# LayerNorm statistics in a one-core streaming encoder step: the variance by a product of ones, rstd from exp(-ln/2) and a Newton step

## What is computed

```
proj   = rms_norm(x) @ W_in                       # 1024 -> 3584, split into h,b,c,z (a) and a,g,z (b)
out_a  = b_a * conv3(c_a * h_a) * silu(z_a)       # 512 channels
conv_b = conv31(a_b * sigmoid(g_b)) + bias        # 512 channels
s_b    = silu(layer_norm(conv_b) * g + b)         # over the 512 channels
y      = x + concat(out_a, s_b * silu(z_b)) @ W_out
return rms_norm(y), and the last rows of both convolutions' inputs
```

## Time and profile before

| what | value |
|---|---|
| median of 3 runs | 1513.71 us (1513.64 to 1514.19) |
| the profiled execution | 1513.34 us |
| its span, first to last instruction | 1511.5 us |
| mean granted TensorE clock | 0.999 of full speed |
| busy: PE, DVE, ACT, POOL | 1500.0, 1306.0, 593.5, 652.7 us |

### The profile page before, as it was taken

The page is one execution under the profiler, slowest core; times in us unless marked ns, Lnnn a source line. Parts: engine busy times, 40 slices in busy tenths (PEclk is TensorE's granted clock), DMA queues, the critical chain, the costliest instruction groups (busy, mean ns, idle before and its releaser), DMA issues.

```text
span 1511.5 us, 19728 instructions
## 1 busy us (share of the span) xinstructions
PE 1500.0 (99%) x7114; PEld 1323.5 (88%) x7114; DVE 1306.0 (86%) x1333; ACT 593.5 (39%) x986; POOL 652.7 (43%) x569
## 2 busy tenths in 40 slices
PE   9999999999999999999999999999999999999998
PEld 8999999988888888888888888889898778888885
DVE  7899999999998898899899895798898788888875
ACT  7553432433342343333253322124444344444433
POOL 4887778311424232342432351116654544444441
PEclk9999999999999999999999999999999999999999
DMA  6897968688988889998789888767867755455541
GB/s 250 308 356 286 366 248 323 213 305 302 319 292 292 278 283 334 306 343 283 257 276 320 299 269 261 247 209 209 247 217 230 257 189 177 169 184 193 171 152 70
DMA packets 119512, 388.97 MB, mean 257 GB/s; under 512 B 17848, under 2 KB 23096, under 8 KB 115832
## 3 DMA queue, kind: packets, MB, share of 16 engines
q1 hardware_dynamic: 116872, 387.57, 74.9%
q10 hardware_dynamic: 2544, 0.14, 0.1%
HBM read 279.19 MB, written 108.47 MB: 256 GB/s over the span
## 4 chain that ended last, share of the span: by engine, by line
PE 97%; DVE 1%; DMA 1%; POOL 0%; issue 0%; ACT 0%; SPq 0%; POOLq 0%; DVEq 0%; ACTq 0%
PE ps L2399 32%; PE ps L2401 32%; PE ps L2400 32%; PE ps L2521 0%; PE ps L2514 0%; DMA conv_b<-conv_spill 0%; DMA x_raw<-in_xT 0%; PE ps L2605 0%; PE ps L2609 0%; DVE conv_b L2177 0%; DVE h_rows_odd L2332 0%; POOL w_ring_f L1302 0%; PE ps L2507 0%; DVE h_rows_even L2325 0%; PE ps L2508 0%
## 5 line engine op out<-in xcount | busy, mean ns | idle before, releaser
L2137 DVE SCALAR_TENSOR_TENSOR ps<-v,conv_b_taps,ps 128x920 f32<-128x920 f32 (+2 forms) x580 | 630.7, 1087 | 17.3
L2399 PE MATMUL ps<-xf,w_ring 128*128 128x460 f32 (+1 forms) x1624 | 603.4, 372 | 0.3 <-issue 0.3
L2401 PE MATMUL ps<-xf,w_ring 128*128 128x460 f32 (+1 forms) x1624 | 603.2, 371 | 0.0
L2400 PE MATMUL ps<-xf,w_ring 128*128 128x460 f32 (+1 forms) x1624 | 601.3, 370 | 0.0
L2399 PEld LDWEIGHTS ps<-xf,w_ring 128*128 128x128 f32 x1624 | 305.6, 188 | 33.9 <-issue 1.1
L2400 PEld LDWEIGHTS ps<-xf,w_ring 128*128 128x128 f32 x1624 | 305.6, 188 | 33.8
L2401 PEld LDWEIGHTS ps<-xf,w_ring 128*128 128x128 f32 x1624 | 305.1, 188 | 33.9
L1598 ACT ACTIVATE sets<-ps 128x460 f32<-128x460 f32 x168 | 92.7, 552 | 477.3 <-PE ps L2401 477.3
L1339 POOL TENSOR_TENSOR w_ring<-w_ring_f,w_ring 128x512 fp32r<-128x512 f32 x28 | 38.8, 1386 | 214.9 <-ACT w_ring L1628 214.9
L2399 PE MATMUL ps<-out_forms,w_ring 128*128 128x512 f32 x288 | 113.9, 396 | 1.4 <-DVE h_rows_even L2325 1.4
L2401 PE MATMUL ps<-out_forms,w_ring 128*128 128x512 f32 x288 | 112.4, 390 | 0.0
(11 more groups left out here) (233 smaller groups left out, 2137.3 us busy)
## 6 DMA issues: line engine op xcount, KB each, us to landing
w_ring<-weight_forms SPq DMA_DIRECT2D x294, 512.0 KB, 5.4
weight_forms<-xf SPq DMA_DIRECT2D x7, 2048.0 KB, 11.6
weight_forms<-w_ring SPq DMA_DIRECT2D x7, 2048.0 KB, 11.4
x_row<-in_x_prompt SPq DMA_DIRECT2D x28, 512.0 KB, 7.5
out_weight_forms<-w_ring SPq DMA_DIRECT2D x28, 512.0 KB, 6.7
w_ring_f<-in_w_in SPq DMA_DIRECT2D x56, 256.0 KB, 3.5
x_raw<-in_xT SPq DMA_DIRECT2D x31, 460.0 KB, 6.9
xf_f<-in_w_in SPq DMA_DIRECT2D x24, 512.0 KB, 6.2
```

Of the source, the lines that this page charges most:

```text
L2137: dve.scalar_tensor_tensor(dst, window, wb[:, j, k:k + 1], part, ALU.mult, ALU.add).then_inc(taps_done, 1)
L2399: pe.matmul(out, ahi, bhi, start=(start and x == 0), stop=False, skip_group_check=goes_on)
L2400: pe.matmul(out, ahi, blo, start=False, stop=False, skip_group_check=goes_on)
L2401: mm = pe.matmul(out, alo, bhi, start=False, stop=(stop and x == len(terms) - 1), skip_group_check=goes_on)
```

## The change

The variance is no longer made by columns. ACT and DVE split the sum of squares into high and low (square_sum_high, square_sum_low), and PE multiplies both by the 1/512 matrix as for the mean (variance). ACT takes Ln of variance plus epsilon and Exp of minus half of it, both over 128x512, and DVE refines the result in three operations (one Newton step). The result lies in SBUF (tb, or for L = 0 the x row), from where normalise reads it, not in PSUM. Slots: high and low in slot 4, variance in 5, rstd and normalise in 7; for L = 1 in 7, 8 and 9, and its silus and gate come one slot earlier. In the late section: low in period 9, variance and rstd in 10.

Small changes: the load of W_out's P4 form is issued ahead of the last spill; for pair 2, P4 of pair 1 and P1 of pair 2 are added within last_lows, and the final scaling of pair 1's rows comes in slot 3; at the end the main part is multiplied ahead of the cross part, the cross part is added last, and ACT makes the last mean square.

```diff
-            def column_rstd(L):                    # POOL
-                pool.tensor_tensor(rstd_cols[:, 0:c], var_cols[:, 0:c], minus_half[:, :].to_broadcast([P, c]),
-                                   ALU.pow).then_inc(ln_cols_rstd, 1)
-            def column_var(L):                     # ACT
-                act.activation(var_cols[:, 0:c], ps[:, STAT_BANK, 0:c], ACT.Identity, scale=1.0 / DA,
-                               bias=ln_eps[:, :]).then_inc(ln_cols_var, 1)
+            def square_sum_high(L):                # ACT
+                act.wait_ge(ln, ln_event(L, "squares"))
+                act.activation(ta_split[:, 1, 0:w], tb[:, 0, 0:w], ACT.Copy).then_inc(ln_var_hi, 1)
+            def rstd_seed(L):
+                act.wait_ge(ln_var, L + 1)
+                act.activation(ln_rstd_places(L)[0], ps[:, STAT_BANK, 0:w], ACT.Ln,
+                               bias=ln_eps[:, :]).then_inc(ln_log, 1)
+                act.wait_ge(ln_log, L + 1)
+                act.activation(ln_rstd_places(L)[0], ln_rstd_places(L)[0], ACT.Exp, scale=-0.5).then_inc(ln_seed, 1)
...
+            def square_sum_low(L):                 # DVE
+                dve.wait_ge(ln_var_hi, L + 1)
+                dve.tensor_tensor(ta_split[:, 0, 0:w], tb[:, 0, 0:w], ta_split[:, 1, 0:w].bitcast(F32),
+                                  ALU.subtract).then_inc(ln_var_lo, 1)
+            def refine_rstd(L):
+                dve.wait_ge(ln_seed, L + 1)
+                dve.scalar_tensor_tensor(t, y, -0.5, y, ALU.mult, ALU.mult).then_inc(ln_step, 1)
+                dve.scalar_tensor_tensor(t, ps[:, STAT_BANK, 0:w], ln_eps[:, :], t, ALU.add, ALU.mult).then_inc(ln_step, 1)
+                dve.scalar_tensor_tensor(y, t, 1.5, y, ALU.add, ALU.mult).then_inc(ln_step, 1)
...
-                rs = ps[:, STAT_BANK, 0:w].unsqueeze(1).to_broadcast([P, JT, w])
+                rs = ln_rstd_places(L)[0].unsqueeze(1).to_broadcast([P, JT, w])
...
-            def column_sums(L):                    # PE, and column_spread(L) alike
-                    mm = pe.matmul(ps[:, STAT_BANK, c:c + 1], tb[:, 0, P * c:P * (c + 1)], ones[:, :],
-                                   start=True, stop=True)
+            def variance(L):
+                pe.wait_ge(ln_var_lo, L + 1)
+                pe.matmul(dst[:, 0:w], mean_w[:, :], ta_split[:, 1, 0:w], start=True, stop=False)
+                pe.matmul(dst[:, 0:w], mean_w[:, :], ta_split[:, 0, 0:w], start=False, stop=True).then_inc(ln_var, 1)
...
-        FIRST_LN_SLOT = {... "square_sums": 6, "columns": 8, "spread": 10, "silus": 11, "gate": 12}
+        FIRST_LN_SLOT = {... "square_sums": 6, "square_sum_parts": 7, "variance": 8, "rstd": 9, "silus": 10, "gate": 11}
-        LN_SLOT = {... "square_sums": 3, "columns": 5, "spread": 7, "silus": 8, "gate": 10}
+        LN_SLOT = {... "square_sums": 3, "square_sum_parts": 4, "variance": 5, "rstd": 7, "silus": 8, "gate": 10}
...
+                if m == 2:                         # DVE, last_lows_of, behind its first sum
+                    add_product(1, P4)
+                    add_product(2, P1)
...
-            spill(PERIODS - 1)
             for s in range(2):
-                sp.wait_ge(spill_ab[s], ab_sent(PERIODS - 2 + s))
-                sp.wait_ge(spill_dc[s], dc_sent(PERIODS - 2 + s))
                 sp.wait_ge(v_state[s], 16 * 4)
             sp.wait_ge(conv_out, conv_sent(JOBS - 1))
+            sp.wait_ge(spill_ab[0], ab_sent(PERIODS - 2))
+            sp.wait_ge(spill_dc[0], dc_sent(PERIODS - 2))
             for e in range(JT):
                 load_out_form(P4, e)
+            spill(PERIODS - 1)
...
-            first_ln = {7: centre, 8: square_sums, 11: normalise}
+            first_ln = {7: centre, 8: square_sums, 9: square_sum_low, 10: refine_rstd, 11: normalise}
```

More of the change, by code:

```diff
@@ L743, in h_part_of @@
             return hrow[m % 2][:, row, DA * half:DA * (half + 1)]
[L745 to L748, removed]
+        FIRST_LN_SLOT = {"sums": 1, "sum_high": 3, "sum_low": 3, "mean": 4, "squares": 5, "square_sums": 6,
+                         "square_sum_parts": 7, "variance": 8, "rstd": 9, "silus": 10, "gate": 11}
+        LN_SLOT = {"sums": -2, "sum_high": -2, "sum_low": -2, "mean": 1, "squares": 2, "square_sums": 3, "square_sum_parts": 4,
+                   "variance": 5, "rstd": 7, "silus": 8, "gate": 10}
         def ln_due(m, i, step):
@@ L1873, in _ @@
             last_square(1)
+            act.wait_ge(last_ms, 1)
+            act.wait_ge(last_sq, 2)
+            act.activation(mean_sq[0:SAMPLE, 2:3], ssq[0:SAMPLE, 1:2], ACT.Identity,
+                           bias=mean_sq[0:SAMPLE, 0:1]).then_inc(last_ms, 1)
             act.wait_ge(last_g, 2)
@@ L2367, in _ @@
                         centre(ln_due(m, i, "mean"))
-                    if m and i in (1, 2):
+                    if m == 2 and i == 3:
+                        finish_rows(1, 0)
+                        finish_rows(1, 1)
+                    elif m and m != 2 and i in (1, 2):
                         finish_rows(m - 1, i - 1)
-                    if ln_due(m, i, "spread"):
-                        normalise(ln_due(m, i, "spread"))
+                    if ln_due(m, i, "rstd"):
+                        refine_rstd(ln_due(m, i, "rstd"))
+                        normalise(ln_due(m, i, "rstd"))
                     if ln_due(m, i, "gate"):
@@ L2562, in _ @@
                 if n == III + 10:
[L2563 to L2565 removed]
+                    variance(0)
                 late_tile(n, 0)
@@ L2604, in sample_product @@
                 for x, (row, i, e) in enumerate(parts):
+                    mm = pe.matmul(ps[0:2 * SAMPLE, main, :], sample_rows[:, row, 0:2 * SAMPLE], out_weights(i, e)[0],
+                                   start=x == 0, stop=x == len(parts) - 1)
+                mm.then_inc(last_half, 1)
+                for x, (row, i, e) in enumerate(parts):
                     mm = pe.matmul(ps[0:SAMPLE, cross, :], sample_rows[:, row, SAMPLE:2 * SAMPLE], out_weights(i, e)[1],
@@ L2607, in sample_product @@
                 mm.then_inc(last_cross, 1)
-                for x, (row, i, e) in enumerate(parts):
-                    mm = pe.matmul(ps[0:2 * SAMPLE, main, :], sample_rows[:, row, 0:2 * SAMPLE], out_weights(i, e)[0],
-                                   start=x == 0, stop=x == len(parts) - 1)
-                mm.then_inc(last_half, 1)
             for m in range(PAIRS):
@@ L2616, in _ @@
                         mean(ln_due(m, i, "mean"))
-                    if ln_due(m, i, "columns"):
-                        column_sums(ln_due(m, i, "columns"))
-                    if ln_due(m, i, "spread"):
-                        column_spread(ln_due(m, i, "spread"))
+                    if ln_due(m, i, "variance"):
+                        variance(ln_due(m, i, "variance"))
                     out_product(m, i)
```

105 lines of the change are left out of this document (52 added, 53 removed).

## The result

The changed kernel takes 1548.94 us (median of 5 runs, 1545.11 to 1550.01), the kernel before 1513.64: slower by 2.3%, ratio 1.0229, 95% interval 1.0218 to 1.0240. The prediction had the side right (slower) and the size wrong: 1528, range 1518 to 1533. The profiled run took 1550.01 us with a span of 1548.2, which is 36.7 more than the 1511.5 of before.

What follows compares the result with a forecast made beforehand. PE (99% busy) was taken as the bound as long as DVE keeps up. 10.2 + 3.9 + 1.6 - 0.3 - 1.0 = +14.4 us on a span of 1511.5 led to a median of 1528, range 1518 to 1533.

Steps and rivals of the forecast that it cites:

- What PE gains: Two 1/512-matrix matmuls (0.46 us) replace column sums and spread (0.90 us each): 1.34 us a group, about 11 us over nine.
- Groups 2 to 7: P6 waits about 3.1 us for P1's addition on DVE; each group 1.7 us longer, 10.2 us in six.
- A: Start of the column work, now variance, in slot 5; P6 was forecast to start at A + 14.6.
- The 0.45 us: Added to normalise's 2.24 us for reading rstd from SBUF beside POOL; a like case went from 1.23 to 1.71.
- Table loads: Three a group, one between Ln and Exp, expected at 1.28 us; without that one, 0.9 us less a group.
- Rival 2: Ln and Exp need one load: 6 x 0.9 us less, about 1522.5 us; chance 0.18, with or without smaller head waits.
- Group 0 (+1.6): Late section: PE waits 2.84 us for the squares' low part, less column work saved; net +1.6 us.
- groups 1 and 2 (+3.9): Late split of squares delays variance(1) by 3.0 us; +3.9 us to variance(2), with group 1's gain and small changes.
- The end (-1.0, group 8 -0.3): Quarter-width group 8 saves PE 0.3 us; one addition (0.79) and ACT's own mean square (about 0.2) save 1.0.
- Rival 1: P6's wait doesn't bind because DVE adds P1 by A + 11.5; PE count holds, about 1502 us; chance 0.09.
- The chances: Own range 1524 to 1533: 0.62; the rivals 0.18, 0.05, 0.09 and 0.04; the rest, 1516 to 1519, 0.02.
- Rival 3: Loads or the operations reading SBUF cost more: 1533 to 1536 us; chance 0.05 above 1533.

Runs made afterwards that it cites:

- seed_p1_first: Changed kernel without the Newton step, Exp writing the seed to PSUM, first two variances later, P1's addition ahead of normalise: 1512.4 us.
- pe_filled: Changed kernel with 14 useless 512-column matmuls put in PE's pause ahead of P6 in odd pairs 3 to 13: 1541.1 us.
- ln_copy: Changed kernel with Copy in place of Exp for the seed, so no table load between the two seed instructions: 1540.6 us.
- no_newton: Changed kernel without the Newton step, normalise taking the seed of Exp as it is: 1523.3 us.
- p1_first: Changed kernel with P1's addition ahead of Newton step and normalise in odd pairs from 3, row scalings and gate later: 1533.5 us.
- psum_rstd: Changed kernel with the third Newton instruction writing the rstd to the statistics' PSUM bank, where normalise reads it: 1541.5 us.
- places: Changed kernel with the first two variances later: group 0's by half a period, group 1's by one product: 1538.6 us.
- seed_places: Changed kernel without the Newton step, Exp writing the seed to PSUM, and the first two variances later: 1506.7 us.
- all_four: Changed kernel with P1's addition first, rstd in PSUM, the two early variances later, and Exp behind P5's and P6's high parts: 1530.2 us.
- newton_gate: Changed kernel, Newton step kept, with P1's addition first, gate behind P7's addition, rstd in PSUM, early variances and pair 1's row scalings later: 1527.3 us.
- small_only: Kernel before with the small changes alone, the variance staying by columns: 1513.7 us.

## Why the prediction was wrong in size

- **What PE gains.** Right: two matmuls by the matrix take the place of the columns, and the one group in which PE hardly waits (the last full one of seed_p1_first) takes 39.1 us, where the prediction had 39.3.
- **Groups 2 to 7, "each group pays anew: 6 x 1.7 = 10.2 us".** This is the step that failed, as a mis-sized term: it was 24.6 us, 4.1 a group. The mechanism, the instruction that waits and its releaser were right. Two things were missing. First, the pause was priced at its own length, and the clock behind it at nothing: the slow matmuls add 1.56 us a group (pe_filled against the changed kernel). Second, P6 came at A + 15.19, not 14.6, and most of these 0.6 us is normalise, taken as 2.69 us and 3.17 in the trace. It waits until POOL's instruction has ended (1342.04) and then needs 2.15 us. The 0.45 us that the prediction added came from the earlier trace rows, read as a fixed surcharge. Beside that row, in the kernel before, stands

```profile
1261.78 1.64 POOL L1345 TENSOR_TENSOR w_ring<-out_a,w_ring 128x512 fp32r<-128x512 f32 x1 [2.39 <-ACT w_ring L1641]
```

which ended 0.63 us after DVE's instruction had started (1262.79) and cost it 0.48; POOL's instruction beside normalise ended 1.10 us after its start and cost 0.96. What counts is how much of POOL's instruction is left. 1.7 + 0.6 + 1.56 leaves about 0.2 us a group unaccounted for.
- **Table loads.** Right in number and place, with 1.28 us each; the second load costs about what I took for it (ln_copy). Rival 2, one load for Ln and Exp, fell: there are nine loads ahead of Ln and nine ahead of Exp. The Trainium skill (ScalarE: Activation LUTs, What ACT_TABLE_LOAD costs) counts 2.66 us for a switch. The trace doesn't bear it out: Exp starts 1.30 us after its load has started.
- **Group 0 (+1.6) and groups 1 and 2 (+3.9).** Together +13.1, the other mis-sized term. Variance(1) waited 4.14 us, as the last part of the prediction said (near 4). Variance(0) waited 4.94, not 2.84: DVE reached the low part at 1131.2, not 1128.3. This place varies: in kernels whose code is the same up to there, it waited 5.3 us (no_newton), 3.1 (ln_copy), 2.0 (p1_first) and 5.5 (psum_rstd), one trace each. Why DVE is at different places in the late section wasn't tried. The run places shows that both waits together are worth 12.5 us, clock and followers included.
- **The end (-1.0, group 8 -0.3).** Right: -1.05 in all.
- **Rival 1 (faster)** named a condition that is not enough: in p1_first P1's addition was in time and P6 didn't wait, and the kernel took 1533.5 us, not 1502. DVE made other products late. The kernel beats the one before, by 0.46% (seed_places), only with the Newton step's 2.2 us out of DVE and the rstd in PSUM. With the Newton step none of the orders tried had a median below 1527.
- **The chances.** All of them together lay at 1536 us or below; nothing was kept for 1548.9. Rival 3 came closest, with 0.05: an operation that reads SBUF did cost more, but by only 0.5 us a group.
- **Open:** whether a better order of DVE, ACT and POOL could hide the Newton step. p1_first, all_four and newton_gate say only that these three don't. Nor is it shown why the same kind of wait lowers the clock in one group and not in the next.

## What to carry to other kernels

A wait of the busiest engine can cost more than its length, because its clock can fall behind it: look for start-to-start steps that nearly double after an idle stretch. A pause of 3.5 us in this kernel cost 5. Moving work from small column operations to full-width ones on an engine with idle time is not free if the work stands in front of the one addition that everything waits for: find that addition first. And a vector instruction with both operands in SBUF should be placed, or given a PSUM operand, so that it doesn't meet the other engine that shares its way there.

## What the runs showed of the hardware

- PE's clock behind a wait between matmuls of 512 columns: after 3.54 us and more it fell every time; after 2.69 and 2.71 us it fell in one group of ln_copy and not in another, and after 1.95 to 1.96 us in two of five groups of newton_gate. After 0.61 us (no_newton) and 1.66 us (the changed kernel) it did not. In small_only it fell after a wait of 1.40 us with one-column matmuls behind it, 2.70 us between full ones. 14 matmuls in the pause kept it.
- DVE instructions with two SBUF inputs and POOL instructions take turns as a whole. Normalise took 2.29 us alone and 3.25 beside a POOL instruction of 1.48; the gate 2.29 alone and 4.40 beside one of 2.39; with one operand in PSUM it was 2.286 in every case. The Trainium skill (SBUF — State Buffer, SBUF: two separate sides) says that the two engines hold a shared pair of ports for a whole instruction and that the other blocks. The rows above agree to about 0.15 us: behind POOL's end, 2.15 us are left of an instruction that takes 2.29 alone.
- Ln followed by Exp loaded a table each time (9 and 9 loads of 1283 ns). The Trainium skill (ScalarE: Activation LUTs, Table sets: the hidden batching unit) has both in one set, with one load. In this kernel, as built, each had a load of its own.
